# Turning x to tokens in the SSD mixer of a hybrid decoder step: by 32x32 blocks on VectorE in place of TensorE's turns

## What is computed

```python
xbc_c, xbc_state = causal_dwconv(xbc, xbc0, ssm_conv_w, ssm_conv_b)
xbc_c = jax.nn.silu(xbc_c)
xs, Bm, Cm = split_last(xbc_c, (D_INNER, SSM_GROUPS * SSM_STATE, SSM_GROUPS * SSM_STATE))
...
y_diag = jnp.einsum('bclgsr,bcsgrp->bclgrp', Wm, x)
chunk_states = jnp.einsum('bclgn,bclgr,bclgrp->bcgrpn', Bm, decay_end * dt, x)
```

## Time and profile before

| | value |
|---|---|
| median of 3 runs | 2827.12 us (2826.7 to 2828.85) |
| the profiled execution, its own time | 2829.19 us |
| its span in the profile | 2827.5 us |
| PE, busy | 2795.7 us (99%) |
| DVE, busy | 1781.7 us (63%) |
| ACT, busy | 1162.6 us (41%) |
| POOL, busy | 295.2 us (10%) |
| DMA, moved | 476.28 MB, mean 168 GB/s |
| mean granted clock of PE | 0.997 |

### The profile page before, as it was taken

One profiled execution on the slowest core, in us unless ns is written; L12 is line 12 of the kernel. 1 busy time (PEld: TensorE's weight loads), 2 busy tenths in 40 slices (PEclk: granted clock), 3 DMA queues, 4 the chain that ended last, 5 costly groups with the idle time before them and its releaser, 6 DMA issues.

```text
span 2827.5 us, 53397 instructions
## 1 busy us (share of the span) xinstructions
PE 2795.7 (99%) x19408; PEld 2758.7 (98%) x19408; DVE 1781.7 (63%) x2244; ACT 1162.6 (41%) x1721; POOL 295.2 (10%) x456
## 2 busy tenths in 40 slices
PE   8899999999999999999999999999999999999998
PEld 7899999999999999999999999999999999999998
DVE  7778878887888655545545556555555555555564
ACT  5454454544544333333333335433333333333553
POOL 2222121222212100000000001000000000000100
PEclk9999999999999999999999999999999999999999
DMA  8787897887878665555555554555555555555463
GB/s 216 191 211 193 209 231 187 198 223 194 216 194 209 180 177 150 148 148 148 149 149 150 148 148 144 155 145 151 149 149 156 150 145 151 148 149 151 134 182 112
DMA packets 901699, 476.28 MB, mean 168 GB/s; under 512 B 158313, under 2 KB 895009, under 8 KB 901297
## 3 DMA queue, kind: packets, MB, share of 16 engines
q1 hardware_dynamic: 827417, 433.14, 56.8%
q10 hardware_dynamic: 73528, 39.39, 5.0%
q0 software_dynamic: 672, 2.66, 0.2%
HBM read 449.62 MB, written 25.47 MB: 168 GB/s over the span
## 4 chain that ended last, share of the span: by engine, by line
PE 95%; DVE 1%; ACT 0%; issue 0%; ACTq 0%; DVEq 0%
PE ps L1732 30%; PE ps L1734 30%; PE ps L1733 30%; PE ps L1976 1%; PE ps L1992 1%; PE ps L1832 1%; PE ps L1874 0%; PE ps L1884 0%; PE ps L1875 0%; PE ps L2110 0%; PE ps L2117 0%; PE ps L2121 0%; PE ps L1983 0%; PE ps L2096 0%; PE ps L1908 0%; PE ps L1823 0%
## 5 line engine op out<-in xcount | busy, mean ns | idle before, releaser
L1732 PE MATMUL ps<-n_hi,whi 128*128 128x320 f32 x4144 | 1286.0, 310 | 2.3 <-DVE wlo L1095 1.6
L1733 PE MATMUL ps<-n_lo,whi 128*128 128x320 f32 x4144 | 1281.0, 309 | 0.0
L1734 PE MATMUL ps<-n_hi,wlo 128*128 128x320 f32 x4144 | 1281.0, 309 | 0.0
L1095 DVE TENSOR_TENSOR wlo<-raw,whi 128x1024 fp32r<-128x1024 f32 x746 | 920.2, 1245 | 470.6 <-ACT whi L729 469.7
L729 ACT ACTIVATE whi<-raw 128x1024 fp32r<-128x1024 f32 x746 | 783.7, 1057 | 832.2 <-PE ps L1734 721.2
L1732 PEld LDWEIGHTS ps<-n_hi,whi 128*128 128x128 f32 x4144 | 778.5, 188 | 5.5 <-DVE wlo L1095 2.2
L1733 PEld LDWEIGHTS ps<-n_lo,whi 128*128 128x128 f32 x4144 | 778.7, 188 | 1.3
L1734 PEld LDWEIGHTS ps<-n_hi,wlo 128*128 128x128 f32 x4144 | 778.5, 188 | 0.0
L1732 PE MATMUL ps<-c_hi,whi 128*128 128x320 f32 x1728 | 535.8, 310 | 1.2 <-DVE wlo L1095 0.5
L1734 PE MATMUL ps<-c_hi,wlo 128*128 128x320 f32 x1728 | 533.9, 309 | 0.0
L1733 PE MATMUL ps<-c_lo,whi 128*128 128x320 f32 x1728 | 533.9, 309 | 0.0
(11 more groups left out here) (301 smaller groups left out, 1767.6 us busy)
## 6 DMA issues: line engine op xcount, KB each, us to landing
raw<-in_w_in SPq DMA_DIRECT2D x322, 512.0 KB, 4.6
raw<-in_w_ffn_gate SPq DMA_DIRECT2D x88, 512.0 KB, 4.6
raw<-in_w_ffn_up SPq DMA_DIRECT2D x88, 512.0 KB, 5.0
raw<-in_w_ffn_down SPq DMA_DIRECT2D x88, 512.0 KB, 4.0
raw<-in_w_ssm_out SPq DMA_DIRECT2D x64, 512.0 KB, 6.1
hs<-in_state_ssm ACTq DMA_DIRECT2D x32, 512.0 KB, 6.2
hq<-in_state_ssm SPq DMA_DIRECT2D x512, 32.0 KB, 3.3
out_ssm_sample<-hs ACTq DMA_DIRECT2D x32, 512.0 KB, 3.6
```

Source lines behind the costliest of these rows:

```text
L1095: tt(wlo[slot][:], raw[slot][:], whi[slot][:].bitcast(F32), SUB).then_inc(lo_split, 1)
L1732: mm(out, w_h, x_h, start=first, stop=False)
L1733: mm(out, w_h, x_l, start=False, stop=False)
L1734: return mm(out, w_l, x_h, start=False, stop=last)
```

## The change

PE's twelve turns at `ssd1` go, with their waits. DVE gets `turn_x`: for tiles lo to hi of x it transposes blocks of 32 channels by 32 tokens from `xs` and writes each block across partitions to its place in banks 2, 3 and 4, where the turns used to put it. One call (three tiles) stands at `x` 5, ahead of its convolution and behind two new waits; the other (the fourth tile) at `ssd1`, ahead of the `xchunk`s. A call is 24 instructions: 16 that write both prompt chunks of a block row, and 8 for the samples' 64 tokens. `xt_done` now counts two per group, and DVE waits for it itself. On ACT the SiLU of unit 4 moves ahead of the copy of unit 5.

```diff
@@ ACT, unit x
                     if seg.start and j == 0:
                         close_pair(g - 1, 3)
+                    if j == 5:
+                        silu_x(g, 4)
                     act.wait_ge(multiplied, unit_end(seg, it, pos))
...
-                    if j:
+                    if 0 < j < 5:
                         silu_x(g, j - 1)
@@ DVE
+            def turn_x(g, lo, hi):
+
+                dve.wait_ge(xs_ready, 6 * g + 2 + hi)
+                for pc in range(4):
+                    src = xs[pc * HB:(pc + 1) * HB, lo:hi, :]
+                    pairs = src[:, :, 0:SEQ].rearrange("p q (c n) -> p q c n", c=2)
+                    for tb in range(4):
+                        rows, cols = slice(tb * HB, (tb + 1) * HB), slice(pc * HB, (pc + 1) * HB)
+                        dst = ps[rows, 2:5, :].rearrange("p c (q n) -> p q c n", q=4)
+                        last = v.transpose(dst[:, lo:hi, 0:2, cols], pairs[:, :, :, rows])
+                        if tb < 2:
+                            last = v.transpose(dst[:, lo:hi, 2, cols], src[:, :, SEQ + tb * HB:SEQ + (tb + 1) * HB])
+                last.then_inc(xt_done, 1)
@@ DVE, unit x
+                    if j == 5:
+                        dve.wait_ge(yo_kept, 2 * g + 1)
+                        wait(dve, out_added, 8 * g)
+                        turn_x(g, 0, 3)
                     if not (seg.name == "ssm" and seg.start == 0 and j == 1):
                         convolve(g, j)
                 elif kind == "ssd1":
                     dve.wait_ge(hcol_ready, g + 1)
                     wait(dve, hfin_stored, 16 * g)
-                    dve.wait_ge(xt_done, 3 * g + 3)
+                    turn_x(g, 3, 4)
+                    dve.wait_ge(xt_done, 2 * g + 2)
@@ PE
-                elif kind == "ssd1":
-                    pe.wait_ge(xs_ready, 6 * g + 6)
-                    wait(pe, vsum_read, g)
-                    if seg.start == 0:
-                        pe.wait_ge(rows_kept, 2)
-                    wait(pe, out_added, 8 * g)
-                    for c in range(3):
-                        rows = P if c < 2 else NS
-                        for q in range(4):
-                            last = turn(ps[0:rows, 2 + c, q * P:(q + 1) * P], xs[:, q, token_rows(c)], ident[:])
-                        last.then_inc(xt_done, 1)
```

## The result

The changed kernel takes 2910.83 us (median of four runs, 2908.71 to 2912.12). The ratio to the kernel before is 1.0293, with a 95% interval of 1.0281 to 1.0305. That is 84 us slower; the forecast was 53 us slower, and the range ended at 2907.

What follows compares the result with a forecast made beforehand. PE, busy nearly throughout, was taken as the bound, with DVE's queue then delaying the pair: 7 x 7.0 + 3.7 = 52.7 us on 2829.19, less 2.07 for the median, gave 2880 us; range 2852 to 2907.

Steps and rivals of the forecast that it cites:

- The edit on PE, and on ACT: At ssd1 PE's twelve turns go, 1.31 us a group, nothing replacing them; on ACT the moved SiLU costs 0.
- Contention with POOL: Sixth convolution and wlo pair, now after POOL's products on hs, take 2.27 and 2.30 us, their quiet times less 0.07.
- T: DVE's time for both transpose calls: 11.9 us a group; 8.7 all overlapping, 13.5 none, about 15.2 with fill.
- Where the written rows change: In DVE's calls, 16 of 24 transposes start 25 ns after the last ends; otherwise 75 ns before its end.
- The pair's start: In the loop's groups the pair starts at 456.7, not 451.35, after PE stands still for about 6 us.
- The step that failed: DVE's 48 transposes a group, priced by duration and spacing: 7.3 us first call, 4.6 us second.
- the lateness neither grows nor is recovered: DVE waits for PE at the next group's outputs as now, so each loop group adds the same 7.0 us.
- Further on PE isn't held again: Behind the pair: DVE's lead at z2 shrinks only from 4.0 to 2.7 us; next wlo pair has 6 us cover.
- 8T - 42.5: Total slowdown over eight groups as a formula in DVE's transpose time per group; 52.7 us forecast.
- The rival of dear transposes: Bank writes, block filling or small queue costs make DVE's transposes 15.2 us a group: 79 us more, 2906; chance 25%.
- The signs: Changed profile: 384 transposes, seven pair waits near 6 us, clock 0.50, convolution 2.3 us, groups 119 us apart, later stages unchanged.
- The clock: After PE's stop the clock falls to 0.50 and the pair block takes 4.65 us, not 3.00: 1.6 added a group.

Runs made afterwards that it cites:

- e3_notrans: Changed kernel with each transpose call replaced by one memset into the same banks, x not turned at all; 2820.16 us, ratio 0.9973.
- e11_silu_back: e5_slot0 with the SiLU of x's third tile back behind the copy of the sixth unit on ACT; 2908.73 us, ratio 1.0285.
- e10_rows_outer: e5_slot0 with turn_x's two loops exchanged, the same transposes in another order; 2892.49 us, ratio 1.0226.
- e1_hint: Changed kernel with a back-edge prefetch hint for DVE's SSM loop and its head at slot 0; 2893.45 us, ratio 1.0235.
- e5_slot0: Changed kernel with the head of DVE's SSM loop placed at slot 0, without the hint; 2892.96 us, ratio 1.0229.
- e4_warm: Changed kernel with 36 unused matmuls on PE ahead of the pair's wait for xwe; 2923.82 us, ratio 1.0347.
- e2_pad: Kernel before with 48 tiny memsets added to each DVE loop iteration, making the body 271 instructions; 2828.21 us, ratio 1.0001.
- e6_pad239: e2_pad with the head of DVE's loop put at slot 239; 2838.25 us, ratio 1.0037.
- e12_one_call: e5_slot0 with one transpose call for all four tiles at ssd1, 24 wider instructions a group instead of 48; 2888.49 us, ratio 1.0216.
- e9_warm24: e5_slot0 with 24 unused matmuls on PE in the loop only, behind one more wait for xt_done; 2898.0 us, ratio 1.0242.

## Why the prediction was wrong, point by point

**Sign and mechanism.** Right: DVE has no gap between the masks and the pair, its queue sets the pair, and the change makes the kernel slower.

**The edit on PE, and on ACT.** Right. e3_notrans gives back 1.3 us a group and nothing more; e11_silu_back shows what the moved SiLU saves.

**Contention with POOL.** Right: 2.2 us for the convolution and 2.35 for the wlo pair, as taken from quiet rows. POOL's products haven't gone: they now meet the wlo pair at 486.07, which takes 3.94 us, behind the pair's start and out of PE's way.

**T.** The mechanism was right: 16 of 24 instructions held, 8 overlapping by 0.08. The size was a little off, 12.8 for 11.9, because the forms with two chunks take 389 and 256 ns instead of 345 and 212 (1.4 us for 32 of them), of which shorter gaps, about 15 ns behind a held instruction instead of 25, give back 0.5; those with one chunk (242 and 175) came as taken from the rows of linear operations. "Where the written rows change" was too narrow a reading of what holds: e10_rows_outer shows that the rows read count too. The Trainium skill, VectorE: DVE Perf Modes, "Two Vector instructions with no wait between them", names input and output, and e10_rows_outer agrees. For the order in this kernel both readings give the same.

**The pair's start.** From the wlo pair's start to the pair the prediction has 456.7 - 433.91 = 22.8 us, the trace 484.00 - 460.28 = 23.7: the difference is that of T. The wait was to be near 6 us (6.3 measured), the block at half clock 4.65 (4.46). The short hold at z1's second half, forecast as 0.5 us and swallowed, is 1.0 us and is swallowed. Group 0: +3.7 forecast, +3.7 measured, through a cancellation of small terms that I wouldn't count on.

**The step that failed** is the edit on DVE: it priced the 48 instructions by their execution alone, and closed with "the lateness neither grows nor is recovered" and "Further on PE isn't held again". But the instructions also have a place in DVE's program. They moved the loop's head from the 171st instruction to the 219th (group 0's 48) and made its body 48 longer, and so each of six back edges costs a stop of 4.2 us. The rows of before could not show that stop, but the sizes of the loop could have been counted. Removing it alone brings 17.4 (e1_hint) or 17.9 us (e5_slot0), a fifth of the whole slowdown.

**The sum again.** With T = 12.8 the prediction's own formula, 8T - 42.5, gives 59.9 us, 7.2 more than the forecast. By spans of the profiled runs e1_hint, free of the back-edge stops, is 2889.6 - 2827.5 = 62.1 us above the kernel before, so 2.2 over the formula. Four of the loop's six steps from pair to pair take 119.8 to 119.9 us, as the formula has it (112.0 and 7.9), the other two 120.4 and 121.8; that makes the 2.2, and what makes these two longer wasn't traced. The step into the loop adds 1.3 and the stretch behind the last pair takes about as much off. The one stop on the way into the loop (3.2 us on DVE) hardly reaches PE: from the pair of group 0 to that of group 1 e1_hint takes 121.5 us, the changed kernel, which has no such stop, 121.1. The changed kernel's span is 18.4 us above e1_hint's. So the spans differ by 80.5 us where 52.7 were forecast, and the 27.8 between are 7.2 from T, 18.4 from the back edges and 2.2 from this rest. The other 3 us of the 31 between the forecast of 2880 and the result are no work in the kernel: the medians lie 83.9 apart and the spans 80.5, because the profiled execution of the kernel before was 2.2 us above its median, which the forecast took off, and because an execution's time exceeds its span by 1.7 us before and 2.7 after. The rival of dear transposes (2906) came near the time for another reason than its own: T was not 15.2.

**The signs.** Of those that the prediction named, the 384 transposes, the seven waits near 6 us, the clock and the sixth convolution came. But it also said that it would be wrong if the groups differ in length, and they do: within the loop they come 122.8 to 124.2 us apart, where it had 119, and the step without a back edge grew by 7.2 us while the others grew by 11.4. That sign points at the back edge.

**The clock.** The fall to 0.50 and the slow block came as forecast. But its price, 1.6 us a group, wasn't had back singly: in e4_warm the period fell by 0.2, as PE then meets DVE at the old outputs. Apart from the back edges, the claim that PE isn't held again was true only because the slow block hid that wait.

## What to carry to other kernels

Before moving work onto an engine inside a loop, count that engine's instructions: how long the body becomes and where its head lies. A stop named "issue" at the head of each iteration and a doubled count of packets in the engine's instruction queue are its signs, and moving the head can cure it (here 17 us for one argument). And weigh the rates: PE turned these tiles in 1.31 us a group; DVE, by 48 blocks that mostly can't overlap, needs 12.8, at the one place of the group where it had 3.3 us of lead.

## What the runs showed of the hardware that was not expected

- A stop at the back edge depends on place: 271 instructions from the 171st on cost nothing (e2_pad), from slot 239 on 3.1 us each time (e6_pad239), from the 219th on 4.2 us (the changed kernel), from slot 0 on nothing at the back edges and 3.1 us once on the way in (e5_slot0).
- Transposes of 32 partitions that span two chunks cost some 45 ns more each than those within one, at the same 1.04 ns a column (e12_one_call).
- DVE's transposes from SBUF into the banks and POOL's products on `hs` don't slow each other here: beside the products (463.24 to 467.29) the wide form takes 0.39 us as it does later, and the four products take 4.05 us, while the convolution's steps beside the same products take twice their time (2.69 for 1.19 us).
- The granted clock had fallen after a stop of PE of 2.53 us (e9_warm24).
- Matmuls added to PE's loop raise the packets of q8 from 51 to 70, and the stretch behind the SSM stage grows by 13.9 us (e4_warm) and 8.0 us (e9_warm24), with waits of PE for "issue" at the weight products. Why wasn't tested; it makes them a poor means to hold the clock.
